# A linear recurrence on one core: chunk products of 128x128 with zero blocks, or pairs of 64x64 blocks

## The reference, cut to what matters

```python
def step(S, inp):                       # S: one 64 x 64 state per head
    r_t, w_t, k_t, v_t, kk_t, a_t = inp
    sa = einsum('bhvk,bhk->bhv', S, -kk_t)
    S = S * w_t[:, :, None, :] + sa[..., None] * (kk_t * a_t)[:, :, None, :] \
        + v_t[..., None] * k_t[:, :, None, :]
    o = einsum('bhvk,bhk->bhv', S, r_t)
    return S, o
```

## Time and profile before

| | |
|---|---|
| timed runs | median 1977.06 us, 1972.89 to 1981.99 |
| profiled execution | 1980.46 us, span 1978.7 us |
| TensorE clock granted | 0.957 on average |
| PE busy | 1870.6 us (95%), 9406 instructions |
| PEld busy | 1580.4 us (80%) |
| DVE busy | 1549.6 us (78%), 1458 instructions |
| ACT busy | 1152.2 us (58%), 1099 instructions |
| POOL busy | 59.4 us (3%) |
| DMA | 489.01 MB, 247 GB/s on average |

### The profile page before, as it was taken

The page is one execution under the profiler, slowest core; times in us unless marked ns, Lnnn a source line. Parts: engine busy times, 40 slices in busy tenths (PEclk is TensorE's granted clock), DMA queues, the critical chain, the costliest instruction groups (busy, mean ns, idle before and its releaser), DMA issues.

```text
span 1978.7 us, 25415 instructions
## 1 busy us (share of the span) xinstructions
PE 1870.6 (95%) x9406; PEld 1580.4 (80%) x9406; DVE 1549.6 (78%) x1458; ACT 1152.2 (58%) x1099; POOL 59.4 (3%) x84
## 2 busy tenths in 40 slices
PE   7989779999997899999999999999999998988998
PEld 7989767887876788888888888888888887777777
DVE  6875566888675779889798897888978886675685
ACT  5632144334464667767677676776767765564554
POOL 2000000110110000000000000000000000000000
PEclk9989599999998799999999999999999999988999
DMA  6301338997421699998999989999999993522421
GB/s 226 128 1 20 78 89 297 319 331 259 156 90 65 255 373 346 361 380 330 375 345 361 376 334 370 349 360 373 338 370 348 362 371 125 159 83 77 155 94 56
DMA packets 162265, 489.01 MB, mean 247 GB/s; under 512 B 8506, under 2 KB 13755, under 8 KB 162064
## 3 DMA queue, kind: packets, MB, share of 16 engines
q1 hardware_dynamic: 153536, 458.21, 63.7%
q0 software_dynamic: 8656, 29.82, 4.7%
HBM read 485.36 MB, written 2.62 MB: 247 GB/s over the span
## 4 chain that ended last, share of the span: by engine, by line
PE 56%; issue 9%; DVE 3%; ACT 1%; DMA 0%; POOLq 0%; POOL 0%; DVEq 0%; ACTq 0%
PE bank L1143 17%; PE bank L1145 17%; PE bank L1144 17%; PE bank L1623 2%; PE bank L1688 1%; DVE weights_at L1893 1%; PE bank L1763 0%; PE bank L1633 0%; PE bank L1634 0%; PE bank L1788 0%; DMA BIG<-in_w_in 0%; DVE x_low L1920 0%; DVE SM L2718 0%; PE bank L1138 0%; ACT weights_at L2829 0%
## 5 line engine op out<-in xcount | busy, mean ns | idle before, releaser
L2475 DVE TENSOR_TENSOR expert_weights_low<-BIG,expert_weights_high 128x2048 fp32r<-128x2048 f32 x336 | 750.6, 2288 | 57.3 <-ACT expert_weights_high L3110 57.0
L3110 ACT ACTIVATE expert_weights_high<-BIG 128x2048 fp32r<-128x2048 f32 x336 | 625.2, 1922 | 65.9 <-DMA BIG<-in_o_moe_up 40.9
L1143 PE MATMUL bank<-expert_weights_high,expert_x_high 128*128 128x512 f32 x896 | 352.1, 393 | 2.4 <-DVE expert_x_low L2540 2.3
L1145 PE MATMUL bank<-expert_weights_low,expert_x_high 128*128 128x512 f32 x896 | 349.6, 390 | 0.0
L1144 PE MATMUL bank<-expert_weights_high,expert_x_low 128*128 128x512 f32 x896 | 349.5, 390 | 0.0
L1893 DVE TENSOR_TENSOR weights_at<-BIG,weights_at 128x2048 fp32r<-128x2048 f32 (+2 forms) x100 | 219.1, 2191 | 84.9 <-ACT weights_at L2829 82.8
L2829 ACT ACTIVATE weights_at<-BIG 128x2048 fp32r<-128x2048 f32 (+2 forms) x100 | 183.6, 1836 | 174.9 <-DMA BIG<-in_e_ffn_down 39.5
L1143 PE MATMUL bank<-weights_at,x_high 128*128 128x512 f32 (+2 forms) x608 | 241.9, 398 | 19.9 <-DVE x_low L1920 7.7
L1145 PE MATMUL bank<-weights_at,x_high 128*128 128x512 f32 (+2 forms) x608 | 237.8, 391 | 0.0
L1144 PE MATMUL bank<-weights_at,x_low 128*128 128x512 f32 (+2 forms) x608 | 237.3, 390 | 0.0
L1143 PEld LDWEIGHTS bank<-expert_weights_high,expert_x_high 128*128 128x128 f32 x896 | 168.7, 188 | 37.0 <-DVE expert_x_low L2540 2.4
(11 more groups left out here) (405 smaller groups left out, 2296.8 us busy)
## 6 DMA issues: line engine op xcount, KB each, us to landing
BIG<-in_o_moe_gate SPq DMA_DIRECT2D x112, 1024.0 KB, 5.1
BIG<-in_o_moe_up SPq DMA_DIRECT2D x112, 1024.0 KB, 5.3
BIG<-in_o_moe_down SPq DMA_DIRECT2D x112, 1024.0 KB, 5.2
BIG<-in_w_ada POOLq DMA_DIRECT2D x48, 512.0 KB, 4.9
BIG<-in_w_in SPq DMA_DIRECT2D x20, 1024.0 KB, 5.0
BIG<-in_o_w_qkv SPq DMA_DIRECT2D x12, 1024.0 KB, 5.1
BIG<-in_e_w_in SPq DMA_DIRECT2D x10, 1024.0 KB, 5.1
BIG<-in_e_ffn_gate SPq DMA_DIRECT2D x10, 1024.0 KB, 5.6
```

The source lines that it names most:

```text
L1143: mm(b, high_l, high_r, start=start, stop=False, skip_group_check=not check)
L1145: last = mm(b, high_l, low_r, start=False, stop=stop, skip_group_check=not check)
L2475: tt_(E_WL[q % E_SLOTS], half(q % E_SLOTS), E_WH[q % E_SLOTS].bitcast(F32), SUB).then_inc(w_low, 1)
L3110: f(E_WH[q % E_SLOTS], half(q % E_SLOTS), ACT.Copy).then_inc(w_high, 1)
```

## The change

Each 128x128 block becomes two 64x64 blocks, one above the other: chunk 0 of the tile on partitions 0 to 63, chunk 1 on 64 to 127, 64 columns in place of 128. A product of two blocks becomes two products on opposite quarters of TensorE's array (rows and columns 0 to 63, rows and columns 64 to 127), issued one behind the other into one bank, on different partitions. The evictions take 256 columns in place of 512.

AB, CB and A are computed per head and chunk, with the heads of even and odd parity in two separate banks, and VectorE masks eight blocks in one instruction. ZV and OV are paired as the inverse is. In the chunk loop the state of a head pair is two 64x64 states above each other; Z and O lie in two banks by the parity of the head, O's part from the state is issued ahead of the wait for `ZS`, and O's two banks are taken at the head of the chunk. dS needs no mask: VectorE adds and scales, in two operations in place of three (in chunk 0 a copy in place of the mask). SA stays one product per head, of half the columns. `twice` signals two banks by one instruction, also in the differential attention, where it stands for a separate increment.

The core of the diff:

```diff
-    for u in range(8):
-        add(("AB", u), "v")
-        add(("CB", u), "v")
-    for u in range(4):
-        add(("A", u), "v")
+    for tt in range(TT):
+        for at, name in enumerate(("AB", "CB")):
+            for q in range(2):
+                add((name, tt, q), "v", 4 * tt + 2 * at + q)
+    for tt in range(TT):
+        for q in range(2):
+            add(("A", tt, q), "v", 2 * tt + q)
...
-        if c:
-            add(("Z", c), "v")
-        add(("SA", c), "v")
-        if c < 3:
-            add(("dS", c), "v")
-        add(("O", c), "a")
+        for q in range(2 if c else 0):
+            add(("Z", c, q), "v", q)
+        add(("SA", c), "v", 2)
+        if c < 3:
+            add(("dS", c), "v", 3)
+        for q in range(2):
+            add(("O", c, q), "a", 4 + 2 * (c % 2) + q)
...
+            def head_blocks(name, tt, lhs, rhs, n):
+                b = [fill(pe, (name, tt, q)) for q in range(2)]
+                for c in range(4):
+                    for q in range(2):
+                        for k in range(2):
+                            r, t = slice(HALF * q, HALF * q + HALF), slice(tt * P + HALF * k, tt * P + HALF * k + HALF)
+                            last = mm(b[q][HALF * k:HALF * k + HALF, c * n:(c + 1) * n], lhs(r, c, t), rhs(r, c, t),
+                                      start=True, stop=True)
+                        if c == 3:
+                            last.then_inc(filled, 1)
...
                     for i in range(4):
-                        last = mm(b[:, i * P:(i + 1) * P], AM[:, 4 * gr + i, :], YI[:, 4 * gr + i, :],
-                                  start=True, stop=True)
+                        for r in chunks:
+                            last = mm(b[r, i * HALF:(i + 1) * HALF], AM[r, 4 * gr + i, :], YI[r, 4 * gr + i, :],
+                                      start=True, stop=True)
...
                     for h in range(8):
-                        last = mm(b[:, h * 64:(h + 1) * 64], CB2[:, at_head(tt, h), w * P:(w + 1) * P],
-                                  TMV[:, tt, h * 64:(h + 1) * 64], start=True, stop=True)
+                        for r in chunks:
+                            last = mm(b[r, h * 64:(h + 1) * 64], CB2[r, at_head(tt, h), w * HALF:(w + 1) * HALF],
+                                      TMV[r, tt, h * 64:(h + 1) * 64], start=True, stop=True)
...
+                out = [fill(pe, ("O", c, q)) for q in range(2)]
                 if c:
                     pe.wait_ge(state_ready, c)
-                    group(("Z", c), state(0))
-                    wait_taken(pe, ("Z", c))
+                    from_state([fill(pe, ("Z", c, q)) for q in range(2)], 0, True, True)
+                    from_state(out, 1, True, False)
+                    wait_taken(pe, ("Z", c, 1))
...
                 if c < 3:
-                    group(("dS", c), [(p * P, P, a[r, tt, p * P:(p + 1) * P], b_[r, p * P:(p + 1) * P])
-                                      for p in range(4) for a, b_ in ((TMK, SAN), (TMT, TMV[:, tt, :]))])
-                group(("O", c), state(1)
-                      + [(h * 64, 64, B1T[r, at_head(tt, h), :], SAN[r, h * 64:h * 64 + 64]) for h in range(8)])
+                    b = fill(pe, ("dS", c))
+                    for p, q, ch, at in heads:
+                        to = b[ch, p * HALF:(p + 1) * HALF]
+                        mm(to, TMK[r, tt, at], SAN[r, at], start=True, stop=False, skip_group_check=True)
+                        last = mm(to, TMT[r, tt, at], TMV[r, tt, at], start=False, stop=True, skip_group_check=True)
+                    last.then_inc(filled, 1)
+                for h, (p, q, ch, at) in enumerate(heads):
+                    last = mm(out[q][r, p * HALF:(p + 1) * HALF], B1T[r, at_head(tt, h), :], SAN[r, at],
+                              start=c == 0 and p == 0, stop=p == 3, skip_group_check=True)
...
+            for tt in range(TT):
+                take(v, ("AB", tt, 1))
+                x = bank[:, 4 * tt * BANK:(4 * tt + 2) * BANK].rearrange("p (i w t) -> p i w t", w=2, t=HALF)
+                V(tt_(YI[:, blocks_of(tt), :], x[:, :, 0, :], bc(cst("join1_up"), 1, [P, 8, HALF]), MUL))
+                V.twice(tt_(B1T[:, blocks_of(tt), :], x[:, :, 1, :], bc(cst("until_chunk"), 1, [P, 8, HALF]), MUL), ev)
+                take(v, ("CB", tt, 1))
+                x = bank[:, (4 * tt + 2) * BANK:(4 * tt + 4) * BANK].rearrange("p (i x) -> p i x", x=P)
+                V.twice(tt_(CB2[:, blocks_of(tt), :], x, bc(pair, 1, [P, 8, P]), MUL), ev)
...
-                    V(tt_(DS, b, bc(cst("same_head"), 1, [P, 4, P]), MUL), ev)
                     if c:
-                        V(tt_(DS, DS, ST[c % 2], ADD))
-                    V(tt_(ST[(c + 1) % 2], DS, bc(s_pl[:, :, c], 2, [P, 4, P]), MUL), state_ready)
+                        V(tt_(DS, b, ST[c % 2], ADD), ev)
+                    else:
+                        V(d.tensor_copy(DS, b), ev)
+                    V(tt_(ST[(c + 1) % 2], DS, bc(s_pl[:, :, c], 2, [P, 4, HALF]), MUL), state_ready)
```

More of the change, by code:

```diff
@@ L81, in const_tables @@
     for s in (1, 2, 4, 8, 16, 32):
[L83 to L84 removed]
+        join = (j // (2 * s) == t // (2 * s)) & (j % (2 * s) >= s) & (t % (2 * s) < s)
+        parts[f"join{s}"] = in_chunk(join)
+        if s == 1:
+            parts["join1_up"] = in_chunk(join.T)
     parts["future"] = np.concatenate([np.zeros((P, P)), np.where(t > j, MASKED, 0.0)], 1)
@@ L496, in __call__, with twice @@
         self.eng.wait_ge(sem, self.made[sem.num])
+    def twice(self, instruction, sem):
+        self.made[sem.num] = self.made.get(sem.num, 0) + 2
+        instruction.then_inc(sem, 2)
+        self.eng.wait_ge(sem, self.made[sem.num])
     def once_more(self, sem):
@@ L1333, in _ @@
             rows_by_token((4, 5, 0, 1, 2, 3))
+            chunks = [slice(0, HALF), slice(HALF, P)]
             for n, s in enumerate(LEVELS):
@@ L1369, in _, with from_state @@
             for c in range(4):
[L1370 to L1380 removed]
+                tt, r = c // 2, chunks[c % 2]
+                t0 = slice(c * HALF, (c + 1) * HALF)
+                heads = [(h // 2, h % 2, chunks[h % 2], slice(h * HALF, (h + 1) * HALF)) for h in range(8)]
+                def from_state(b, w, start, stop):
+                    for p, q, ch, at in heads:
+                        last = mm(b[q][r, p * HALF:(p + 1) * HALF], QR[ch, p, w, t0], ST[c % 2][ch, p, :],
+                                  start=start and p == 0, stop=stop and p == 3, skip_group_check=True)
+                        if stop and p == 3:
+                            last.then_inc(filled, 1)
+                out = [fill(pe, ("O", c, q)) for q in range(2)]
                 if c:
                     pe.wait_ge(state_ready, c)
[L1383 to L1384 removed]
+                    from_state([fill(pe, ("Z", c, q)) for q in range(2)], 0, True, True)
+                    from_state(out, 1, True, False)
+                    wait_taken(pe, ("Z", c, 1))
                 else:
@@ new lines, in blocks_of @@
+            def blocks_of(tt):
+                return slice(8 * tt, 8 * tt + 8)
+            for tt in range(TT):
+                take(v, ("AB", tt, 1))
[5 more added lines that the diff above has]
+                V.twice(tt_(CB2[:, blocks_of(tt), :], x, bc(pair, 1, [P, 8, P]), MUL), ev)
@@ new lines, in _ @@
+            for tt in range(TT):
+                q = blocks_of(tt)
+                take(v, ("A", tt, 1))
+                x = bank[:, 2 * tt * BANK:(2 * tt + 2) * BANK].rearrange("p (q x) -> p q x", q=2)[:, :, 0:4 * HALF]
+                after = cst("after_chunk").unsqueeze(1).unsqueeze(1).broadcast_to([P, 2, 4, HALF])
+                V.twice(tt_(AL[:, q, :].rearrange("p (q c) t -> p q c t", q=2),
+                            x.rearrange("p q (c t) -> p q c t", c=4), after, MUL), ev)
+                V(tt_(XI[:, q, :], AL[:, q, :], bc(cst("join1"), 1, [P, 8, HALF]), MUL))
+                V(tt_(XI[:, q, :], bc(cst("ident_chunk"), 1, [P, 8, HALF]), XI[:, q, :], SUB))
+                V(tt_(YI[:, q, :], bc(cst("ident_chunk"), 1, [P, 8, HALF]), YI[:, q, :], SUB))
+                join(LEVELS[0], 2 * tt)
+                join(LEVELS[0], 2 * tt + 1)
@@ L2937, in _ @@
                 r = slice(64 * (c % 2), 64 * (c % 2) + 64)
-                A(f(OO[r, c // 2, :], take(act, ("O", c))[r, :], ACT.Copy), ea)
+                take(act, ("O", c, 1))
+                at = (4 + 2 * (c % 2)) * BANK
+                by_parity = bank[r, at:at + 2 * BANK].rearrange("p (q x) -> p q x", q=2)[:, :, 0:4 * HALF]
+                A.twice(f(OO[r, c // 2, :].rearrange("p (c q t) -> p q c t", q=2, t=HALF),
+                          by_parity.rearrange("p q (c t) -> p q c t", c=4), ACT.Copy), ea)
                 if c == 1:
```

110 lines of the change are left out of this document (44 added, 66 removed).

## The result

The changed kernel takes 1925.55 us (median of 4 runs) where the kernel before takes 1977.17 beside it: 51.6 us less, ratio 0.9737, 95% interval 0.9709 to 0.9765. The forecast was 1938 with a range of 1924 to 1968. The direction was right and the time lies in the range, 1.6 us above its lower end; the gain was larger than the 39 us of the sum, and one wait that was forecast is not there. The profiled execution took 1928.03 us, its span 1926.2.

What follows compares the result with a forecast made beforehand. TensorE was taken to bound the inverse and ZV/OV, with neither engine full in scores and chunk loop. Terms -13.4 - 14.6 - 2.1 + 0.8 - 9.8 = -39 us gave 1938 us, range 1924 to 1968.

Steps and rivals of the forecast that it cites:

- The pace, 0.040 us: New 64 by 64 products: time per instruction, taken between 0.028 (side by side) and 0.057 (one after the other).
- Scores, -13.4: First AB to first dY: 13.4 us saved, with ScalarE late next; 5.6 saved without overlap.
- stops being late: Scores: VectorE's work falls from 27.6 to 13.1 us, so it no longer holds up the stage.
- Inverse, -14.6: Inverse by doubling: groups of 0.64 us, levels of 7.7 us, 34.0 us for 48.6; -17.8 at pace 0.028.
- the fourth U would wait for its join no longer: Inverse: the join comes 1.5 us behind dX, with 1.9 us of U before it, so no wait.
- ZV/OV and the new wait: Chunk values: -2.1 us; then +0.8 us as SA(0) waits for ScalarE's eviction of OV(1).
- Chunk loop, -9.8: SA(0) to group norm: shorter SA, dS and VectorE work, less a loss of 1.1 in the last part; -8 to -11.5.
- a new wait for the root: Chunk loop's last part: VectorE's scan starts 4.0 us late, waiting for ScalarE's root behind O(1)'s eviction; a loss of 1.1.
- The lower clock (1): Products side by side but at 1.2 GHz: inverse only -2.1, total -24, or 1953 us; chance 0.20.
- its serial form (3): Products one after the other and the clock falls, from the inverse's first level: +39, or 2016 us; chance 0.09.
- No overlap in one bank (2): No overlap in one bank or at all, clock kept: pace 0.057, total -12.5, or 1964 us; chance 0.12.
- That the gain would not pass on (4): The path behind the recurrence does not follow, so no change can be told: 1977 us; chance 0.07.

Runs made afterwards that it cites:

- the joins put ahead: Changed kernel with all four joins of the next level made at the head of a level, into a second buffer: 1919.08 us, ratio 0.9707, inverse 26.0 us.
- the old width: Changed kernel with the inverse's joins and evictions of dY, dX and U walking over 512 elements a partition as before: ratio 0.9837, inverse 47.1 us.
- the old time of TensorE alone: Changed kernel with each product of U, dY and dX in the inverse issued twice, evictions still halved: ratio 0.9829, inverse 50.4 us.
- the kernel timed again: The changed kernel itself, word for word, timed beside later edits on the same chip: 1922.61 us, ratio 0.9713 to the kernel before.
- column halves apart: Changed kernel with AB, CB and A issued on array column half 0 first, then half 1: their 192 instructions take 5.53 us, against 4.8.

## Why the prediction was right, and where its sizes were not

The measured gain of the stage (52.4 us) is more than the forecast's with all its good ends (46, or 1930). The range reached 6 us further down, to 1924, without a term behind it, so that the time fell into it at all is in part luck.

*The pace, 0.040 us: mis-sized, at 0.029, and AB and CB at 0.026 where I had 0.055.* The text had both ends and took the middle for fear of the issue of twice as many instructions. The end worked out from full overlap (0.028) was measured in U, dY, dX and ZV/OV. In AB, CB and A the text let the row halves alone overlap, but the column halves do too, and A went at 0.015. The earlier trace rows had come close to full overlap already. The Trainium skill (TensorE: Matmul & The Clock Gate, Back-to-back issue gap) gives an issue floor of about 25 ns for up to 64 columns. This trace does not agree where four quarters take turns: A's instructions, 64 columns each, start every 0.015 us on the mean, so what I held back for issue was not due.

*Scores, -13.4 against -15.5.* The step was right that ScalarE is late next: its token rows end at 113.77 and the first U's eviction follows at 113.81. AB, CB and A took 4.8 us where I had 9.6, but only 2.0 of the 4.8 us saved reach the first dY. That VectorE "stops being late" was not right: the gates wait 2.14 us for its second mask of CB (103.22), and ScalarE's chain of gates and rows starts from there.

*Inverse, -14.6 against -18.8.* The level of 6.78 us is the 6.8 that the text gave for the pace of 0.028, with VectorE late, not the 7.7 that it took. That the fourth U would wait for its join no longer was wrong: the last two wait, 1.0 us a level together, and the joins put ahead took those waits away. What the text did not say is that the halved evictions carry the gain as much as the products do: the old width alone leaves 47.1 us (some 44 without the drop of the clock there, by the estimate above), the old time of TensorE alone 50.4.

*ZV/OV and the new wait, -1.3 against -2.5.* The wait was right in place and size (0.91); the rest is the pace again.

*Chunk loop, -9.8 against -15.7. The step that failed is "a new wait for the root"*: the text has the root rightly behind O(1), and O(1) 0.8 us behind the second state (164.77 and 165.57), but then lets the scan start from that same state. The scan follows the third state, 11.58 us later. Putting the root behind O(2), the place that fits the text's reckoning, gave the wait, 3.56 us of the 4.0 predicted, so the price was right and the place was not. The last part gained 3.0 us where a loss of 1.1 was forecast. That VectorE's low parts, and not O(3), end the stage was right (187.15 to 191.80, no wait for ScalarE). The remaining 1.9 us: dS takes 1.73 us and not 3.0 (1.0 and 0.6 us between the states), and chunk 0 0.25 less.

*The rivals.* The lower clock (1) and its serial form (3) are out for this kernel: the granted clock was 1.00 throughout scores, inverse and ZV/OV. In the kernel timed again it was 0.50 for 2.8 us of the gates, and 1.00 in the inverse as well. It was 0.85 in the scores of before, and 0.52 in the chunk loop against 0.53. With the old width, where TensorE waits longer, it did fall in the inverse. No overlap in one bank (2) is out at 0.029 us per instruction, half of SA's 0.057. The rule of the Trainium skill behind it (TensorEngine Tiling (Array Packing), Restrictions and Gotchas: different row tiles cannot access one bank at the same time) does not show here: two products on different row tiles, into one bank on different partitions, overlapped in full at 0.029. No experiment tried different row tiles on the same partitions of one bank. That the gain would not pass on (4) is out by the timed medians: 51.6 us less, of a stage that is 52.4 shorter. The 1735.2 and 1734.4 us behind the group norm agree better than they need to, since that part differs by up to 21 us between profiled executions.

## What to carry to other kernels

Give both ends of an unmeasured price and name the row that tests it, then believe that row: the attention's scores had shown, nearly, the full overlap that the new products reached. Where TensorE and VectorE are nearly level in a pipelined stage, halving the work of one is worth little (1.5 us and nothing here) and halving both takes off much more (18.8 of 48.6), so count both before an edit and look for the wait that remains afterwards (here a join behind evictions). Read the granted clock of an experiment's own stretches before its times are compared: the old width lost some of its time to a clock of 0.50, and not to its width. Before pricing a wait between two engines, write down on which pass of the loop each end stands; one state off was 4 us.

## What the hardware showed that I had not expected

- Two 64x64 fp32 products side by side need only one half, row or column, to differ: row halves alone 0.027 us per instruction (two banks; the last of A in "column halves apart"), both different 0.029 (one bank), against SA's 0.057 on one quarter; column halves alone 0.053 at the clock of 0.50 (dS, one bank), against 0.104 for SA(1) there ((1.78 - 0.22) / 15). Four quarters by turns give 0.015, a quarter of SA's, so all four run at once.
- Products of different quarters overlap also where they are not neighbours: a change of quarter saved 0.13 to 0.17 us, 2 to 3 instructions, so blocks of 8 on one quarter kept about three quarters of the gain of strict turns: (0.91 - 0.57) of (0.91 - 0.47).
- TensorE's clock stayed granted at 1.00 through the 30 us of the inverse, with half-filled products and waits of 0.20 and 0.83 us a level. With the old width, behind waits of up to 1.5 us for joins, it fell to 0.50 in parts of the inverse. In the chunk loop it was 0.50 from dS(0) on (150.90), ahead of which TensorE had waited 0.91 us for ScalarE and 0.85 for VectorE.
